# Two ways to finish the differential heads of a transformer block: norm across the partitions, or along the channels with a transpose behind it

## The reference

```
def diff_attn_core(q, k, v, lam):
    s = einsum('bqhmd,bkhmd->bhmqk', q, k) * (B_HEAD_DIM ** -0.5)
    p = softmax(s, axis=-1)
    a = p[:, :, 0] - lam * p[:, :, 1]
    return einsum('bhqk,bkhd->bqhd', a, v)

def b_post(o, z, length):
    o = rms_norm(o, subln_w, SUBLN_EPS) * (1.0 - lam_init)
    return o.reshape(bsz, length, B_WIDTH) * silu(z)

out_l = concatenate([a_branch(...), b_post(ob_l, bz_l, seq)], axis=-1) @ w_out
```

## Time and profile before

| | |
|---|---|
| median of 3 runs | 1070.79 us |
| lowest and highest run | 1070.55 and 1072.16 us |
| span of the profiled execution, first to last instruction | 1069.9 us |
| the median less this span | 0.9 us |
| mean granted TensorE clock, share of full speed | 0.997 |

### The profile page before, as it was taken

How to read it: one execution, slowest core, us unless ns; L and a number is a source line. 1 busy time by engine, 2 the same in 40 slices (tenths; PEclk the granted TensorE clock), 3 DMA queues, 4 the chain that set the end, 5 groups by cost and what they waited for, 6 DMA issues and landing times.

```text
span 1069.9 us, 18034 instructions
## 1 busy us (share of the span) xinstructions
PE 1049.8 (98%) x6797; PEld 884.3 (83%) x6797; DVE 733.3 (69%) x1577; ACT 591.8 (55%) x1209; POOL 2.6 (0%) x10
## 2 busy tenths in 40 slices
PE   5999999999999999999999999999999999999997
PEld 3677776788997779989898988889988898888886
DVE  4635567665588756787778766658788778765665
ACT  4534245543364446568776764445567677665444
POOL 0000000000000000000000000000000000000000
PEclk9999999999999999999999999999999999999999
DMA  9998551222342224564555566666464545555662
GB/s 326 336 311 245 181 184 41 60 60 75 83 135 55 78 78 126 140 175 138 138 141 155 145 170 182 193 196 177 129 171 139 139 139 157 157 162 177 194 213 83
DMA packets 203551, 165.41 MB, mean 155 GB/s; under 512 B 7101, under 2 KB 172713, under 8 KB 203465
## 3 DMA queue, kind: packets, MB, share of 16 engines
q1 hardware_dynamic: 202944, 163.28, 52.0%
q0 software_dynamic: 192, 0.66, 0.2%
q10 hardware_dynamic: 328, 0.32, 0.1%
HBM read 163.18 MB, written 1.05 MB: 153 GB/s over the span
## 4 chain that ended last, share of the span: by engine, by line
PE 89%; DVE 7%; ACT 2%; issue 1%; DMA 1%; SPq 0%; ACTq 0%; DVEq 0%
PE pj L2059 23%; PE pj L2061 22%; PE pj L2060 22%; DVE w_lo L1328 2%; PE pj L2153 2%; PE tr L2611 1%; PE ac L2415 1%; PE ac L2550 1%; PE sc L2259 1%; PE tr L2266 1%; PE sc L2401 1%; ACT w_hi L835 1%; PE ac L2280 1%; PE sc L2532 1%; PE sc L2530 1%
## 5 line engine op out<-in xcount | busy, mean ns | idle before, releaser
L1328 DVE TENSOR_TENSOR w_lo<-raw,w_hi 128x1024 fp32r<-128x1024 f32 (+2 forms) x258 | 309.4, 1202 | 148.7 <-ACT w_hi L835 147.8
L835 ACT ACTIVATE w_hi<-raw 128x1024 fp32r<-128x1024 f32 (+2 forms) x258 | 268.0, 1040 | 89.3 <-PE pj L2061 87.3
L2059 PE MATMUL pj<-h_hi,w_hi 128*128 128x256 f32 (+1 forms) x960 | 299.0, 311 | 0.2
L2061 PE MATMUL pj<-h_hi,w_lo 128*128 128x256 f32 (+1 forms) x960 | 291.1, 303 | 0.0
L2060 PE MATMUL pj<-h_lo,w_hi 128*128 128x256 f32 (+1 forms) x960 | 291.0, 303 | 0.0
L2059 PEld LDWEIGHTS pj<-h_hi,w_hi 128*128 128x128 f32 x960 | 183.7, 191 | 19.1 <-issue 10.4
L2061 PEld LDWEIGHTS pj<-h_hi,w_lo 128*128 128x128 f32 x960 | 183.8, 191 | 7.4
L2060 PEld LDWEIGHTS pj<-h_lo,w_hi 128*128 128x128 f32 x960 | 184.0, 192 | 6.2
L2059 PE MATMUL pj<-w_hi,h_hi 128*128 128x512 f32 x344 | 137.4, 399 | 0.4 <-DVE h_lo L1402 0.4
L2061 PE MATMUL pj<-w_hi,h_lo 128*128 128x512 f32 x344 | 134.2, 390 | 0.0
L2060 PE MATMUL pj<-w_lo,h_hi 128*128 128x512 f32 x344 | 134.2, 390 | 0.0
(11 more groups left out here) (358 smaller groups left out, 1473.4 us busy)
## 6 DMA issues: line engine op xcount, KB each, us to landing
raw<-in_w_in_dram SPq DMA_DIRECT2D x152, 512.0 KB, 3.7
ada_raw<-in_ada_w_dram SPq DMA_DIRECT2D x48, 512.0 KB, 7.9
raw<-in_even_w_in_dram SPq DMA_DIRECT2D x28, 512.0 KB, 5.0
raw<-in_w_branch_dram SPq DMA_DIRECT2D x24, 512.0 KB, 3.7
raw<-in_w_out_dram SPq DMA_DIRECT2D x16, 512.0 KB, 3.7
raw<-in_odd_w_in_dram SPq DMA_DIRECT2D x11, 512.0 KB, 3.9
raw<-in_even_w_out_dram SPq DMA_DIRECT2D x8, 512.0 KB, 3.7
raw<-in_odd_w_out_dram SPq DMA_DIRECT2D x8, 512.0 KB, 3.8
```

The costliest lines, as they stand in the source:

```text
L835: last = nc.scalar.activation(hi, src, ACT.Copy)
L1328: last = nc.vector.tensor_tensor(lo, src, hi.bitcast(F32), ALU.subtract)
L2059: nc.tensor.matmul(dst, lh, rh, start=first, stop=False)
L2061: return nc.tensor.matmul(dst, ll, rh, start=False, stop=final)
```

## The change

The operands of the product with the values are swapped in l0_values: the transposed probabilities are now the stationary operand and the values the moving one, so that a unit's result has its tokens as partitions and the channels along the row. The squares' sum is then a reduction along the row, done by VectorE (head_sum, 128x512 to 128x4, at the end of slots 22, 23, 24 and 25). 1/rms is computed as before, at the end of slots 23 and 25, and VectorE scales both heads of the pair with it (head_scale), one factor for each token and head. TensorE then transposes the scaled heads (turn_heads, four 128x128 transposes for each head, in slots 24 and 26, after three quarters of the projection). ScalarE copies them with the gain, which goes by partitions as before, and VectorE multiplies them with the gate (head_end). head_sums, head_rows and head_gate are gone, with them the copies of the sums to SBUF and two uses of the banks tr.

```
--- before.py
+++ after.py
@@ -236,10 +236,8 @@
 LAM_SLOT = 9
 LN_STAT, LN_RSTD, LN_APPLY, MIX_SLOT, WS_SLOT = 6, 9, 10, 13, 7
 HEAD_SQUARE = {20: 0, 22: 1, 24: 2, 25: 3}
-HEAD_STAT = {23: 0, 25: 1}
-HEAD_SPREAD = {24: 0, 26: 1}
-HEAD_RSQRT = (24, 25)
-HEAD_GATE = {24: (0, 1), 26: (2, 3)}
+HEAD_SUM = {22: 0, 23: 1, 24: 2, 25: 3}
+HEAD_TURN = {24: 0, 26: 1}
 HEAD_END = {25: (0, 1), 27: (2, 3)}
 NMIX = 4
 
@@ -312,10 +310,8 @@
     out = [(-1, ("vec", 0))] + [(-1, ("x", k)) for k in range(KT)]
     for s in range(L0_IN + L0_DRAIN):
         out += [(s, ("p", u)) for u in L0_UNITS.get(s - 1, [])]
-        if s in HEAD_STAT:
-            out.append((s, ("hs", HEAD_STAT[s])))
-        if s in HEAD_SPREAD:
-            out += [(s, ("hr", 2 * HEAD_SPREAD[s] + e)) for e in range(2)]
+        if s in HEAD_TURN:
+            out += [(s, ("ht", 2 * HEAD_TURN[s] + e)) for e in range(2)]
         if s == WS_SLOT:
             out += [(s, ("ws", 0)), (s, ("ws", 1))]
     for s in range(L1_IN + 1):
@@ -558,7 +554,7 @@
         pr_set, m_hi_set, m_lo_set = sem("pr_set"), sem("m_hi_set"), sem("m_lo_set")
         sc_done, max_set, exp_set, prob_set = sem("sc_done"), sem("max_set"), sem("exp_set"), sem("prob_set")
         pv_done, o_set = sem("pv_done"), sem("o_set")
-        hs_sq, hs_col, hs_gated = sem("hs_sq"), sem("hs_col"), sem("hs_gated")
+        hs_sq, hs_sum, hs_scaled = sem("hs_sq"), sem("hs_sum"), sem("hs_scaled")
         subln = small[:, 56:57]
         lat_tmp, lat_hi, lat_lo, lat_sq, lat_rs = (
             sem("lat_tmp"), sem("lat_hi"), sem("lat_lo"), sem("lat_sq"), sem("lat_rs"))
@@ -933,8 +929,6 @@
                         act.wait_ge(pv_done, i - 1)
                     nk = TOK if i % 4 < 2 else SEQ
                     turned(use, prob_t[:, i % 2, 0:nk], src[:, 0:nk])
-                elif kind == "hs":
-                    turned(use, lnst[:, 3, :], src[:, 0:8])
                 else:
                     act.wait_ge(prob_set, 16)
                     if i >= 2:
@@ -1003,7 +997,7 @@
                     h = HEAD_SQUARE[s]
                     act.wait_ge(o_set, 4 * h + 4)
                     if h >= 2:
-                        act.wait_ge(tr_done, TR1_OF[("hs", 0)] + 1)
+                        act.wait_ge(hs_sum, h - 1)
                     nc.scalar.activation(scr[:, h % 2, :], o_e[:, h, :], ACT.Square).then_inc(hs_sq, 1)
                 for i in L0_SPLITS.get(s, []):
                     product_hi(i)
@@ -1030,7 +1024,7 @@
                     nc.scalar.activation(small[:, 34:36], small[:, 32:34], ACT.Exp).then_inc(lam_exp, 1)
                 if units:
                     l0_exp(units[-1])
-                while TURNS1[n_turn][0] == s and TR1[n_turn][0] in ("hs", "hr"):
+                while TURNS1[n_turn][0] == s and TR1[n_turn][0] == "ht":
                     l0_turned(n_turn)
                     n_turn += 1
             for m in range(KT + 1):
@@ -1553,23 +1547,27 @@
                 nc.vector.tensor_tensor(m_lo[:, cols], prod_e[:, n % NMIX, :], m_hi[:, cols].bitcast(F32), ALU.subtract)\
                     .then_inc(m_lo_set, 1)
 
-            def head_rsqrt(j):
-
-                dve.wait_ge(tr_free, TR1_OF[("hs", j)] + 1)
+            def head_sum(h):
+
+                dve.wait_ge(hs_sq, h + 1)
+                squares = scr[:, h % 2, :].rearrange("p (i d) -> p i d", i=4)
+                nc.vector.tensor_reduce(lnst[:, 3, 4 * (h % 2):4 * (h % 2) + 4], squares, AX_X, ALU.add).then_inc(hs_sum, 1)
+
+            def head_scale(j):
+
+                dve.wait_ge(hs_sum, 2 * j + 2)
                 v, term, y, sums = (lnst[:, r, :] for r in range(4))
                 after(nc.vector.tensor_scalar(v, sums, 1.0 / P, LN_EPS, ALU.mult, ALU.add))
-                column_rsqrt(y, v, term).then_inc(hs_col, 1)
-
-            def head_gate(h):
-
-                dve.wait_ge(hs_sq, h + 1)
-                nc.vector.tensor_tensor(o_e[:, h, :], o_e[:, h, :], gate_b[h], ALU.mult).then_inc(hs_gated, 1)
+                after(column_rsqrt(y, v, term))
+                for h in (2 * j, 2 * j + 1):
+                    factor = y[:, 4 * (h % 2):4 * (h % 2) + 4].rearrange("p (i a) -> p i a", a=1).broadcast_to([P, 4, P])
+                    o = o_e[:, h, :].rearrange("p (i d) -> p i d", i=4)
+                    nc.vector.tensor_tensor(o, o, factor, ALU.mult).then_inc(hs_scaled, 1)
 
             def head_end(h):
 
-                dve.wait_ge(tr_free, TR1_OF[("hr", h)] + 1)
-                dve.wait_ge(hs_gated, h + 1)
-                nc.vector.tensor_tensor(product_place(4 + h), o_e[:, h, :], expd[:, h % 2, :], ALU.mult).then_inc(pr_set, 1)
+                dve.wait_ge(tr_free, TR1_OF[("ht", h)] + 1)
+                nc.vector.tensor_tensor(product_place(4 + h), expd[:, h % 2, :], gate_b[h], ALU.mult).then_inc(pr_set, 1)
 
             for s in range(L0_IN + L0_DRAIN):
                 if s == LAM_SLOT:
@@ -1587,10 +1585,6 @@
                     product_lo(i)
                 for h in HEAD_END.get(s, ()):
                     head_end(h)
-                if s == HEAD_RSQRT[0]:
-                    head_rsqrt(0)
-                for h in HEAD_GATE.get(s, ()):
-                    head_gate(h)
                 if s == LN_STAT:
                     dve.wait_ge(value_free, 4)
                     for n in range(4):
@@ -1632,8 +1626,10 @@
                     split_lo(s + AHEAD)
                 if units:
                     l0_normalise(units[-1])
-                if s == HEAD_RSQRT[1]:
-                    head_rsqrt(1)
+                if s in HEAD_SUM:
+                    head_sum(HEAD_SUM[s])
+                    if HEAD_SUM[s] % 2:
+                        head_scale(HEAD_SUM[s] // 2)
             dve.wait_ge(*freed_at(G1_OF[("adat", 19)], None))
             modulation(1, 0, KT, 10)
             for m in range(KT + 1):
@@ -2277,30 +2273,18 @@
                 if u >= 1 and u == slot_units(L0_UNITS, u)[0]:
                     pe.wait_ge(o_set, u)
                 for j, n in enumerate(tiles):
-                    last = nc.tensor.matmul(ac[:, P * i:P * i + P], v_e[:, n, P * h:P * h + P], prob_t[:, u % 2, P * j:P * j + P],
+                    last = nc.tensor.matmul(ac[:, P * i:P * i + P], prob_t[:, u % 2, P * j:P * j + P], v_e[:, n, P * h:P * h + P],
                                             start=(j == 0), stop=(j == len(tiles) - 1))
                 last.then_inc(pv_done, 1)
 
-            def head_sums(j):
-
-                use = TR1_OF[("hs", j)]
-                pe.wait_ge(hs_sq, 2 * j + 2)
-                turn_bank(use)
-                for n in range(8):
-                    last = nc.tensor.matmul(tr[:, use % 2, n:n + 1], scr[:, n // 4, P * (n % 4):P * (n % 4) + P], ones[:, 0:1],
-                                            start=(n == 0), stop=(n == 7))
-                last.then_inc(tr_done, 1)
-
-            def head_rows(j):
-
-                pe.wait_ge(hs_col, j + 1)
+            def turn_heads(j):
+
                 for h in (2 * j, 2 * j + 1):
-                    use = TR1_OF[("hr", h)]
+                    use = TR1_OF[("ht", h)]
+                    pe.wait_ge(hs_scaled, h + 1)
                     turn_bank(use)
                     for i in range(4):
-                        n = 4 * (h % 2) + i
-                        last = nc.tensor.matmul(tr[:, use % 2, P * i:P * i + P], lnst[:, 2, n:n + 1].broadcast_to([P, P]), ident,
-                                                start=True, stop=True)
+                        last = nc.tensor.transpose(tr[:, use % 2, P * i:P * i + P], o_e[:, h, P * i:P * i + P], ident)
                     last.then_inc(tr_done, 1)
 
             for s in range(L0_IN + L0_DRAIN):
@@ -2325,15 +2309,10 @@
                     condition(ADA_OF_SLOT[s])
                 for u in L0_UNITS.get(s - 1, []):
                     l0_turn_probs(u)
-                if s in HEAD_STAT or s in HEAD_SPREAD:
-                    project(s, part=(0.0, 0.5))
-                    if units:
-                        l0_scores(units[1])
-                    if s in HEAD_STAT:
-                        head_sums(HEAD_STAT[s])
-                    else:
-                        head_rows(HEAD_SPREAD[s])
-                    project(s, part=(0.5, 1.0))
+                if s in HEAD_TURN:
+                    project(s, part=(0.0, 0.75))
+                    turn_heads(HEAD_TURN[s])
+                    project(s, part=(0.75, 1.0))
                 elif s < L0_IN and len(units) == 2:
                     project(s, part=(0.0, 0.5))
                     l0_scores(units[1])
```

## The result

The changed kernel takes 1064.3 us (median of 4 runs, 1064.25 to 1064.73), the one before 1070.67 in the same comparison (4 runs, 1070.23 to 1072.16). The ratio is 0.9933, 95% interval 0.992 to 0.9947: the kernel is faster, by 0.7%. The forecast said 1065.5 and a gain of 5.3 us. The medians give 6.4, the ratio 7.2 (1070.79 x 0.9933 = 1063.6, just under the range's lower end of 1063.9). The direction was right, and the size too small.

What follows compares the result with a forecast made beforehand. TensorE, packed without a gap while the four heads are finished, was taken to bound the kernel. Removing 7.01 us and adding 1.70 nets 5.3; 1070.79 - 5.3 = 1065.5 us, range 1063.9 to 1067.7.

Steps and rivals of the forecast that it cites:

- What leaves TensorE: Four blocks of small matmuls between the projections, 6.92 us, and a break in slot 25, 0.09: 7.01 us removed.
- What comes: Two turns of eight 128x128 transposes on TensorE, 0.85 us each from start to start: 1.70 us added.
- The swap of operands at nothing: Product with the values on TensorE, operands swapped: the same two instructions each, so no cost; bound 0.1 us per slot.
- VectorE in time: VectorE's 2.4 us of extra work stays hidden before the two turns, with slack 2.6, 2.35, 1.6 and 1.4 us.
- (b): VectorE late at the turns, gain holds in part: scalings of 2 us make TensorE wait 1.6, 1067.1 us; chance 0.05.
- (c): VectorE's scalings read the broadcast operand many times slower: at 3.6 us each the kernel takes 1073.5 us; chance 0.03.
- (e): TensorE transposes issue as two passes, like other f32 matmuls: 2 x 1.70 us, 1067.2 us; chance 0.02.
- Nothing is given back behind the stretch: From 262 us on everything starts 5.3 us earlier; no stage there is pinned to its own time.
- (d): Gain taken back later, at the stages of 295 to 330 us where VectorE is nearly full: 1070.8 us; chance 0.04.
- 1070.79 - 5.3: Final sum: median of the earlier runs less the net saving on TensorE, giving 1065.5 us; chance 0.80.
- (f): Clock falls behind each turn, 1068.7 us, chance 0.02; last half: stretch at 438 us goes or doubles, 1.6 us, 0.04.
- the rival with the clock: The 1.2 GHz stretch at 438 us goes or comes twice: 1063.9 or 1067.1 us; chance 0.04.

Runs made afterwards that it cites:

- e8: Changed kernel with eight more 128x512 VectorE reductions ahead of each pair's second sum; median 1073.67 us of 10, 8.9 above the changed kernel.
- e1: Changed kernel, unedited, timed again beside the kernel before; median 1064.79 us against 1071.60.
- e9: Changed kernel, unedited, timed once more beside the kernel before; median 1064.78 us against 1071.59.
- e4: Kernel before with TensorE's four small blocks cut by 44 instructions; 1064.5 and 1064.97 us without the half-clock stretch, 1066.61 and 1067.62 with it.
- e7: Kernel before with the spreading of one head of each pair done twice; median 1072.42 us of 11 against 1071.03, ratio 1.0011.
- e12: Changed kernel with the turns after half of the projection instead of three quarters; median 1065.58 us of 4 against 1064.78.
- e11: Changed kernel with every transpose of the two turns done five times, 64 more; mean 1071.9 us, none of 11 executions with the half-clock stretch.

## Why the prediction was right and where it was wrong

**What leaves TensorE**: right. 6.92 us of blocks and one break; by the starts after, the parts are 1.81, 1.79 (with the break) and two blocks of 1.70 and 1.71 replaced.

**What comes**: 2 x 0.85 was taken, 2 x 0.79 came. In the eight transposes at 211 from which I read it the first weight load had waited 0.33 us for VectorE, so that the second transpose starts 0.17 us behind the first, where the others follow at 0.11; in the turns all follow at 0.11. A net of 5.3 became 5.4.

**The swap of operands at nothing**: right, 0.80 against 0.81 us.

**VectorE in time**: right. The turns were put at 224.7 and 237.5 and the scalings' ends at 222.1, 222.8, 235.9 and 236.5; less the 0.7 us by which this execution was ahead, they came within 0.3 us. The slack forecast as 2.6, 2.35, 1.6 and 1.4 was 2.3, 2.1, 1.4 and 1.2, and e8 showed it to be what decides. Rivals (b) and (c) fell with one row, 688 ns for a scaling with a broadcast factor; (e) with the x8 of L2287, two heads of four transposes each. (The x112 that the prediction sets against (e) is the count of L2266 in the page's groups, which no rows show.)

**Nothing is given back behind the stretch**: right. Rival (d) has no case for it, the gain of 5.4 is whole at the end.

**Where it failed** is the end of that same step, "1070.79 - 5.3". It took the time before as one level and the change as a pure subtraction, with the term of the clock at nothing. The kernel before has a mean clock of 0.997 or less in 28 of 54 executions, which are 2.1 to 2.2 us longer, and its median mixes the two kinds; the changed kernel has none in 15. In place of 5.3 the comparisons e1 and e9 show 5.5 and 5.3 without the stretch and 6.8 between the medians. The stretch stood in the earlier trace rows, it was named as the last half of rival (f), it was priced right at 1063.9 (1.45 in the trace against "at most 1.6"), and it was given a chance of 0.04. A shift can change the share of a stretch that only part of the executions have; 0.04 was far too small. Of the 7.6 us between the two profiled spans 5.4 are the change's instructions, 1.45 the clock, 0.7 the opening. Of the 6.8 between the medians of e1 and e9 5.4 are the instructions, and the other 1.4 is the share of executions with the stretch.

The first comparison, by itself, does not show as much. The clocks of its executions before are not on record, and three of its four take 1070.23 to 1070.79, where those without the stretch lie (mean 1070.4). The four of the changed kernel lie 0.35 under the mean of the eleven that came later, 1064.75. The ratio puts the time at 1063.6, 0.3 us under the range, and how much of that is the stretch and how much the spread of a few executions stays open. That the median alone, 1064.3, lies within the range is no merit of the sum, whose own case ended at 1065.0: the lower end came from the rival with the clock.

**What stays open.** Why one moment gives the stretch and another not. The order by moment (0, 3.5, 7.0 none; 1.75, 5.25, 5.45 about half or more) was borne out by one forecast. But e4 at 0.47 (two of four) and e7 at 7.24 (four of eleven) had it too, close to moments that have none, as one execution of e12's four at 0.30 us may have, and I cannot say how wide the safe moments are. The additional length of the executions with a mean clock of 0.995 was not seen in any profile.

## What to carry to other kernels

On an engine without a gap, count instructions from start to start: a f32 product cost 0.21 us in this stream and a transpose 0.107 whatever they computed (eight products took 1.70 to 1.81 us, eight transposes 0.79), so a product with one column of ones is as dear as a full one, and work of that kind is better given to an engine with room, if its results come in time for a place late in a slot. Before trusting a difference of medians, look at the mean granted clock of every execution: split by it, e1 and e9 gave 5.5 and 5.3 us, where the medians gave 6.8. And look for a stretch at the lower clock in the profile before: any change ahead of it may take it away or bring it back, so the forecast has to carry both levels.

## What the runs showed of the hardware

- A stretch at the 1.2 GHz level came behind a place at which TensorE had only been idle for 0.25 us and then ran sixteen instructions of one column. It cost 1.45 us. With all that lies before it 1.75, 3.49, 5.25 and 6.99 us longer, four of 5, none of 6, five of 10 and none of 11 executions had it.
- Behind a wait of 3.3 us (e8) a stretch of the same length appeared at once, with the same cost. Behind the wait of 2.3 us before it the clock stayed at 1.00.
- A second operand of VectorE that repeats one number over 128 elements in f32: 688 ns for 128x512, against 682 for a plain one. A reduction of 128x512 f32 from SBUF to four numbers per row: 680 ns, as one to a single number from PSUM (686).
- Transposes did not lower the clock in these lengths: blocks of 8 to 40 in a row (e11) ran at 1.00. The Trainium skill says, in "TensorE: Matmul & The Clock Gate", Part 4: PE-mode transpose, that they do not count as work for the clock gate; no run here shows that.
